# Big products ordered chunk by chunk, so that neighbouring ones write different PSUM banks, in a two-layer hybrid decoder

## The chip, the cores and the metric

The kernel runs on one core of a Trainium2 chip. The metric is the time of one execution on the device in microseconds (us); where several runs are given it is their median.

## What is computed

Two layers over 512 tokens of width 1024, in float32. Each adds to `x` a mixer, a cross attention into 256 memory tokens, and an MLP of hidden width 4096:

```python
for l in range(DEPTH):                      # DEPTH = 2
    h = rmsnorm(x, norm_mix[l])
    x = x + hybrid_mixer(h, w_in[l], ...)   # four branches, gated, w_branch, w_out
    h = rmsnorm(x, norm_xattn[l])
    x = x + cross_attention(h, rmsnorm(mem, norm_mem[l]), w_q, w_kv, w_o)
    h = rmsnorm(x, norm_mlp[l])
    x = x + sq_relu_mlp(h, mlp_w1[l], mlp_w2[l])
return rmsnorm(x, norm_final)
```

Inside the mixer, `h @ w_in` gives the inputs of four token mixers (mLSTM, GLA, S5, HGRN2) and 4096 columns of gates; each branch output is multiplied by its `w_branch`, gated, and summed, and the sum goes through `w_out`. Almost all arithmetic is in the dense products with these weights.

## The kernel before

**Blocks, units, products.** Every dense product is cut into blocks of 256 output columns (`r_f`, `m_o`, `gate2_3`, `q3`, `down3_3` and so on; `block_order` fixes their order). A block over 1024 input rows has four units, a `branch` block (256 input rows) has one. A unit is one DMA of 256 input rows x 256 columns of weights into a ring of nine places. To keep float32 accuracy, each operand is split into a high and a low part: ScalarE (ACT) writes the high part of the weights (line 1135), GpSimd (POOL) subtracts to get the low part (lines 564 and 565), and three products are added: high x high, high weights x low activations, low weights x high activations. A unit holds two chunks of 128 input rows, `k` 0 and 1.

**Banks.** A block accumulates in a set of two PSUM banks, `G[s][0]` and `G[s][1]`; blocks alternate between the two sets (`psum_set`, line 236). In the usual form (`fm`) bank 0 holds output columns 0 to 127 of the block and bank 1 the columns 128 to 255, each with 512 tokens: 12 products of 128x512 per unit, 6 per bank. In the `tm` form (`r_i`, `g_v`, `m_v`, and `kv4` to `kv7`) the activations are stationary, the product is 128x256, and there are four regions of 128 tokens in two banks (two regions for the memory's 256 tokens). `narrow` has a single region.

**The order in `parts` (line 575).** The generator waits for the free set (`gemm_free`, line 581), and in every unit for the weights (`split_ready`). Before: outermost the region `reg`, then the chunk `k`, then the three products. So in the last unit of a block bank 0 gets its last product 6 products before the block's end in `fm` (12 in `tm` over 512 tokens), and `gemm_done` is raised for it there; bank 1's is raised by the last product. Where activations are still being made, `ready` is waited for per chunk, in region 0.

**Who takes the result.** Readers wait for `gemm_done[s]` at `2*used + b + 1`, first b = 0 and then b = 1, and then free the bank: ACT in `banks` (line 1190), `tanh_out` and `gate`, VectorE (DVE) in `merge` (line 1633), in the merge of the fourth branch (line 2058), in `residual` (line 2081) and in `up`. ACT and DVE work through one order written out by hand; ACT also makes the high parts of coming weight units there (`feed_past`, five units ahead of the block's end), and every ACT and DVE instruction waits for the one before it (`chained`). The places that the prediction's steps touch:

- `r_f`: lines 1301 to 1306. ACT copies a bank and takes its absolute value (two instructions per bank), then works on both halves together.
- `m_o`: lines 1378 to 1381, one tanh per bank, followed by the level exponential that a long DVE stretch needs.
- The fourth branch's merge, lines 2058 to 2078: per bank a product with the gate and an addition to `MG`, then two subtractions; ACT makes `MHhi` between them (line 1486). PE runs `branch2_0`, `branch2_1`, `branch2_2` in a row and then `gate2_3`.
- `q3`: line 1515, one copy per bank, then the exponentials of head 0, then `kv_copy(7)`, for which PE waits.
- `down3_3` of the last layer: `residual` adds each bank to `X`, ACT squares and scales (lines 1147 and 1160), DVE sums the squares, and PE's last small products (line 1102 and `norm_tokens`) follow.

Of the kernel before, what the change touches and what calls it, by code (L numbers as in the profile page):

```python
# [13 lines left out]
P = 128  # L14
# [16 lines left out]
BW = 256  # L31
# [104 lines left out]
NARROW = 80  # L136


def units_of(name):
    return 1 if name.startswith("branch") else 4  # L140
# [36 lines left out]
def build(nc, ins, out):  # L177
# [7 lines left out]
    with ctx:  # L185
        def sb(name, shape, dt=F32):
            return ctx.enter_context(nc.sbuf_tensor(name, shape, dt))
# [10 lines left out]
        WLo = nc.alloc_sbuf_tensor_at("w_lo", [P, RING, UW], F32R, offset=ring_at)  # L198
        WHi = sb("w_hi", [P, RING, UW], F32R)
# [33 lines left out]
        def of_layer(s, count):  # L233
            return s, count + now[0] * PER_LAYER[s.name]

        def psum_set(name):
            n = now[0] * NBLOCK + BLOCK[name]
            return n % 2, n // 2

        def first_unit(name):  # L240
            return now[0] * NUNIT + UNIT[name]

        G = [[ctx.enter_context(nc.psum_tensor(f"gemm{s}{b}", [P, 512], F32)) for b in range(2)] for s in range(2)]
# [10 lines left out]
        def sem(name):  # L254
            return ctx.enter_context(nc.semaphore(name))
# [9 lines left out]
        split_hi, split_ready, unit_used = sem("split_hi"), sem("split_ready"), sem("unit_used")  # L265
        gemm_done = [sem(f"gemm_done{i}") for i in range(2)]
# [302 lines left out]
        def _(pe):  # L569
            def mm(o, w, a, start=True, stop=True):  # L570
                return pe.matmul(o, w, a, start=start, stop=stop, skip_group_check=True)  # L571


            def parts(name, hi, lo, kind="fm", n=SEQ, ready=None, ready_at=0):

                s, used = psum_set(name)
                if used:  # L580
                    pe.wait_ge(gemm_free[s], 2 * used)
                u0, units, kcs = first_unit(name), units_of(name), 2
                for un in range(units):
                    u = u0 + un
                    wide = NARROW if kind == "narrow" else BW
                    w_at = lambda W, k, c, m: W[:, u % RING, k * wide + c:k * wide + c + m]
                    nt = {"fm": 2, "tm": n // P, "narrow": 1}[kind]
                    first = True
                    for reg in range(nt):
                        for k in range(kcs):  # L590
                            kc = kcs * un + k
                            if ready is not None and reg == 0:
                                pe.wait_ge(*of_layer(ready, ready_at + kc + 1))
                            if first:
                                pe.wait_ge(split_ready, u + 1)
                                first = False
                            last = kc == kcs * units - 1
                            if kind == "fm":
                                o = G[s][reg][:, 0:n]
                                ops = ((w_at(WHi, k, reg * P, P), hi(kc)), (w_at(WHi, k, reg * P, P), lo(kc)),  # L600
                                       (w_at(WLo, k, reg * P, P), hi(kc)))
                                start = kc == 0
                                ends = last
                            elif kind == "narrow":
                                o = G[s][0][0:NARROW, :]
                                ops = ((w_at(WHi, k, 0, NARROW), hi(kc)), (w_at(WHi, k, 0, NARROW), lo(kc)),
                                       (w_at(WLo, k, 0, NARROW), hi(kc)))
                                start = kc == 0
                                ends = last
                            else:  # L610
                                per = 2 if nt == 4 else 1
                                o = G[s][reg // per][:, (reg % per) * BW:(reg % per) * BW + BW]
                                tok = slice(reg * P, reg * P + P)
                                ops = ((hi(kc)[:, tok], w_at(WHi, k, 0, BW)), (lo(kc)[:, tok], w_at(WHi, k, 0, BW)),
                                       (hi(kc)[:, tok], w_at(WLo, k, 0, BW)))
                                start = kc == 0 and reg % per == 0
                                ends = last and reg % per == per - 1
                            for q, (a, b) in enumerate(ops):
                                i = mm(o, a, b, start=start and q == 0, stop=last and q == 2)
                            if ends:  # L620
                                i.then_inc(gemm_done[s], 2 if kind == "narrow" else 1)

                    if un < units - 1:
                        i.then_inc(unit_used, 1)
                    yield
# [9 lines left out]
            def gemm(*args, **kind):  # L635
                rest(parts(*args, **kind))
# [95 lines left out]
            def gate_parts(n, c):  # L732
                return parts(f"gate{n}_{c}", *H)
# [9 lines left out]
            def x_columns(t, ks, bank):  # L743
                for k in ks:
                    i = pe.transpose(bank(k)[:, t * P:(t + 1) * P], Rf(2 * t + k // 4, 1)[:, (k % 4) * P:(k % 4 + 1) * P], ident)
                return i
# [30 lines left out]
            for L in range(DEPTH):  # L777
                now[0] = L
                block = parts("r_i", *U, kind="tm", ready=u_ready)
                some(block, 2 if L else 1)  # L780
                if L == 0:
                    for k, (s, count) in ((6, (u_hi, 1)), (7, (p_vec, 3))):
                        pe.wait_ge(s, count)
                        for t in range(TT):
                            i = x_columns(t, (k,), XB)
# [86 lines left out]
                for t in range(TT):  # L872
                    i = pe.transpose(M[0][:, t * 64:(t + 1) * 64], R(23)[0:64, 0, t * P:(t + 1) * P], ident[0:64, 0:64])
# [12 lines left out]
                for hp in range(2):  # L886
                    mm(M[hp][:, :], ident, bc(neg_mask, 1, 8), stop=False)
                    for j in range(2):
                        for a in range(2):
                            i = mm(M[hp][64 * a:64 * a + 64, j * 256:j * 256 + 256], head_sel[0:4, 2 * j + hp, :], bm[:, :, a, :],  # L890
                                   start=False, stop=j == 1)
                    i.then_inc(ms["mex_done"], 1)
                for h in range(4):
                    rows = slice(64 * (h % 2), 64 * (h % 2) + 64)
                    for c in range(NCH):
                        tok = slice(c * CH, c * CH + CH)
                        at_ = (h // 2) * 256 + (c // 2) * CH
                        i = mm(M[2 + h % 2][64 * (c % 2):64 * (c % 2) + 64, at_:at_ + CH], MQK[2 + h // 2][rows, tok], MQK[h // 2][rows, tok])
# [3 lines left out]
                for j in range(2):  # L902
                    for t in range(TT):
                        i = pe.transpose(M[j][:, t * P:(t + 1) * P], MQK[2 + j][:, t * P:(t + 1) * P], ident)
# [5 lines left out]
                for h in range(4):  # L910
                    rows = slice(64 * (h % 2), 64 * (h % 2) + 64)
                    for c in range(NCH):
                        p0 = 64 * (c % 2)
                        bank = M[2 * (c % 2) + h // 2]
                        at_ = (c // 2) * 128
                        w = MKT[p0:p0 + 64, c // 2, h // 2, h % 2, :]
                        mm(bank[rows, at_:at_ + 64], w, MV[p0:p0 + 64, c // 2, HD * h:HD * h + HD])
                        i = mm(bank[rows, at_ + 64:at_ + 128], w, ones64[p0:p0 + 64, :])
# [6 lines left out]
                for part in (1, 0):  # L925
# [6 lines left out]
                    for j in range(2):  # L932
                        for c in range(1, NCH):
                            for hp, rows in halves:
                                i = mm(M[2 * part + j][rows, c * CH:(c + 1) * CH], MS[j][rows, c - 1, 64 * part:64 * part + 64],
                                       MQT[rows, j, c * CH:(c + 1) * CH], start=False, stop=True)
# [9 lines left out]
                for r in range(2):  # L946
                    for f in range(2):
                        i = pe.transpose(M[0][:, (2 * r + f) * P:(2 * r + f + 1) * P], R(24 + r)[:, 0, f * P:(f + 1) * P], ident)
                i.then_inc(ss["ct_done"], 1)
                pe.wait_ge(*of_layer(head_rs, 12))  # L950
                for n in range(8):
# [4 lines left out]
                    for t in range(2):  # L956
                        for q in range(2):
                            i = pe.transpose(M[1 + n % 3][:, (2 * t + q) * P:(2 * t + q + 1) * P],
                                             flat(XP[:, r, 4 * q:4 * q + 4, t0 + t, :]), ident)
# [4 lines left out]
                for f in range(2):  # L964
                    for u in range(8):
                        for i4 in range(4):
                            t = 4 * f + i4
                            for r in range(2):
                                i = mm(kk[32 * i4:32 * i4 + 32, f, u, :], XP[:, r, u, t, :], CT[:, r, 32 * t:32 * t + 32],
                                       start=r == 0, stop=r == 1)  # L970
# [8 lines left out]
                un = UU[:, :, :].rearrange("p f (j n) -> p f j n", j=S5_T)  # L979
                for t in range(8):  # L980
                    for r in range(2):
                        at_ = (2 * (t // 4) + r) * 64
                        for q in range(2):
                            for a in range(2):
                                half = slice(64 * a, 64 * a + 64)
                                i = mm(M[t % 4][half, at_:at_ + 64], BT[:, t, r, q, half], U4[:, t, q, :], start=q == 0, stop=q == 1)
# [8 lines left out]
                for f in range(2):  # L995
                    for d in range(S5_T):
                        mm(M[f][:, d * 64:512], KTm[:, f, d, :], flat(un[:, f, 0:S5_T - d, :]), start=d == 0, stop=False)
                    for j in range(S5_T):
                        for i4 in range(4):
                            t = 4 * f + i4  # L1000
                            for r in range(2):
                                i = mm(M[f][32 * i4:32 * i4 + 32, j * 64 + 1:j * 64 + 64], CL[:, r, j, t, :], SX[r][:, t, 0:63],
                                       start=False, stop=r == 1)
# [4 lines left out]
                for n in range(4):  # L1008
                    for k in range(2):
                        i = mm(M[n][:, :], WGLU[:, k, n * P:(n + 1) * P], GE[:, k, :], start=k == 0, stop=k == 1)  # L1010
# [97 lines left out]
            for t in (0, 1):  # L1108
                n = DEPTH * NBLOCK - 2 + t
# [1108 lines left out]
```

## Time and profile before

| | |
|---|---|
| runs | 2127.38, 2127.94, 2133.14 us; median 2127.94 |
| profiled execution | 2130.14 us |
| its span | 2128.3 us, mean granted TensorE clock 0.989 |
| TensorE products | 13631, busy 96% of the span |
| weight loads (PEld) | 13631, busy 79% |
| VectorE, ScalarE, GpSimd | busy 43%, 43%, 49% |

"Busy" of PE counts pipelined products, so that one in flight hides the gap to the next; the distance from start to start is what a stream of products costs. The chain that ended last shows what the end of the span rests on; idle time of an engine matters only where this chain passes it. All products issued through the helper `mm` carry line 571, so they are told apart by their tiles.

### The profile page before, as it was taken

What the parts mean: (1) busy time and instruction counts of PE and PEld (TensorE: products, weight loads), DVE (VectorE), ACT (ScalarE), POOL (GpSimd) and SP (SyncE); (2) the same over time, 40 slices, a digit from 0 to 9 for tenths busy, and PEclk for the clock granted to TensorE, in tenths of its full rate; (3) what the DMA queues carried; (4) which work ended last, traced back from release to release, by engine and by line L of the source; (5) the groups of instructions that cost most, each with busy time, mean ns of one, the idle gap of its engine ahead of it and who ended that gap; (6) DMA issues with size and microseconds to landing.
All of it is one profiled execution on the core that took longest, in us unless ns stands there. A gap on an engine that the chain in (4) does not pass through costs nothing.

```text
span 2128.3 us, 34224 instructions
## 1 busy us (share of the span) xinstructions
PE 2052.3 (96%) x13631; PEld 1689.1 (79%) x13631; DVE 905.7 (43%) x1382; ACT 920.7 (43%) x1568; POOL 1036.7 (49%) x1364
## 2 busy tenths in 40 slices
PE   5999999899999999999999999999999999999998
PEld 4888778777986888888887887777789878888887
DVE  4665765835204321212256576677350243212212
ACT  5655344334445443323356535352345444423323
POOL 2644444444762455456456435426357435555462
PEclk8999999999999999999999999999999999999999
DMA  4322222323431333333333232213224213333332
GB/s 155 98 78 71 75 70 74 86 71 97 135 117 45 94 95 99 97 97 99 95 89 86 67 81 70 69 47 109 85 95 145 94 57 93 99 95 98 97 97 75
DMA packets 205243, 191.21 MB, mean 90 GB/s; under 512 B 30266, under 2 KB 202780, under 8 KB 204700
## 3 DMA queue, kind: packets, MB, share of 16 engines
q1 hardware_dynamic: 205084, 189.02, 30.1%
q8 instruction: 108, 1.77, 0.3%
q14 instruction: 51, 0.42, 0.1%
HBM read 184.77 MB, written 3.15 MB: 88 GB/s over the span
## 4 chain that ended last, share of the span: by engine, by line
PE 83%; DVE 6%; ACT 4%; SPq 3%; issue 1%; POOL 1%; DMA 1%; DVEq 0%; ACTq 0%
PE gemm L571 75%; PE mix L571 7%; SPq L544 2%; DVE work L1593 2%; DVE work L1584 1%; ACT w_hi L1135 1%; DMA small<-in_s_log_step_dram 1%; POOL w_lo L565 1%; DVE work L1680 1%; POOL w_lo L564 0%; DVE work_split L1593 0%; ACT work L1509 0%; DVE merged L1584 0%; SPq L513 0%; DMA w_raw<-in_w_branch_dram 0%
## 5 line engine op out<-in xcount | busy, mean ns | idle before, releaser
L564 POOL TENSOR_TENSOR w_lo<-w_raw,w_hi 128x256 fp32r<-128x256 f32 (+1 forms) x680 | 541.8, 797 | 1064.1 <-ACT w_hi L1135 1063.7
L571 PE MATMUL gemm<-work_split,w_hi 128*128 128x512 f32 (+1 forms) x2048 | 604.5, 379 | 4.7 <-POOL w_lo L565 3.1
L571 PE MATMUL gemm<-h_hi,w_hi 128*128 128x512 f32 (+1 forms) x1456 | 579.6, 398 | 15.5 <-POOL w_lo L565 13.7
L571 PE MATMUL gemm<-h_lo,w_hi 128*128 128x512 f32 (+1 forms) x1456 | 569.2, 391 | 0.0
L571 PE MATMUL gemm<-h_hi,w_lo 128*128 128x512 f32 (+1 forms) x1456 | 568.6, 391 | 0.0
L565 POOL TENSOR_TENSOR w_lo<-w_raw,w_hi 128x256 fp32r<-128x256 f32 (+1 forms) x680 | 543.6, 799 | 0.0
L1135 ACT ACTIVATE w_hi<-w_raw 128x512 fp32r<-128x512 f32 (+1 forms) x680 | 384.3, 619 | 266.3 <-DMA w_raw<-in_mlp_w_dram 186.5
L571 PEld LDWEIGHTS gemm<-work_split,w_hi 128*128 128x128 f32 x2048 | 377.9, 190 | 78.0 <-issue 5.8
L571 PE MATMUL gemm<-work_split,w_lo 128*128 128x512 f32 (+1 forms) x1024 | 386.8, 378 | 0.0
L571 PEld LDWEIGHTS gemm<-h_hi,w_hi 128*128 128x128 f32 (+1 forms) x1456 | 273.6, 188 | 82.4 <-POOL w_lo L565 13.6
L571 PEld LDWEIGHTS gemm<-h_hi,w_lo 128*128 128x128 f32 (+1 forms) x1456 | 273.8, 188 | 59.3
L571 PEld LDWEIGHTS gemm<-h_lo,w_hi 128*128 128x128 f32 (+1 forms) x1456 | 274.0, 188 | 58.0 <-issue 2.4
L571 PEld LDWEIGHTS gemm<-work_split,w_lo 128*128 128x128 f32 x1024 | 194.1, 190 | 35.8
L1584 DVE TENSOR_TENSOR x_t<-x_t,gemm 128x512 f32<-128x512 f32 x96 | 66.0, 688 | 363.4 <-PE gemm L571 362.4
L1584 DVE TENSOR_TENSOR work<-work 128x512 f32<-128x512 f32 (+6 forms) x152 | 127.5, 839 | 69.9 <-ACT work L1226 30.9
L571 PEld LDWEIGHTS mix<-work 64*64 64x64 f32 (+4 forms) x4448 | 114.2, 129 | 38.4 <-issue 31.0
L571 PE MATMUL mix<-work 64*64 64x64 f32 (+6 forms) x4448 | 135.3, 227 | 9.4 <-DVE work L1680 5.1
L1593 DVE SCALAR_TENSOR_TENSOR gate_t<-gemm,work 128x512 f32<-128x512 f32 x64 | 44.3, 692 | 183.5 <-PE gemm L571 165.8
L1559 ACT ACTIVATE gate_t<-gate_t 128x512 f32<-128x512 f32 x64 | 40.5, 632 | 189.1 <-DVE gate_t L1593 189.1
L571 PE MATMUL gemm<-w_hi,work_split 128*128 128x256 f32 x384 | 85.0, 289 | 19.2 <-POOL w_lo L565 19.2
L1220 ACT ACTIVATE gate_t<-gemm 128x512 f32<-128x512 f32 x56 | 33.5, 598 | 124.2 <-PE gemm L571 122.5
L1593 DVE SCALAR_TENSOR_TENSOR work_split<-gate_t,work_split 128x512 fp32r<-128x512 f32 x64 | 46.3, 723 | 91.4 <-ACT work_split L1560 91.4
(278 smaller groups left out, 1674.2 us busy)
## 6 DMA issues: line engine op xcount, KB each, us to landing
w_raw<-in_mlp_w_dram SPq DMA_DIRECT2D x256, 256.0 KB, 2.7
w_raw<-in_w_in_dram SPq DMA_DIRECT2D x224, 256.0 KB, 2.8
w_raw<-in_xattn_w_kv_dram SPq DMA_DIRECT2D x64, 256.0 KB, 2.9
w_raw<-in_w_branch_dram SPq DMA_DIRECT2D x32, 256.0 KB, 2.7
w_raw<-in_w_out_dram SPq DMA_DIRECT2D x32, 256.0 KB, 2.7
w_raw<-in_xattn_w_q_dram SPq DMA_DIRECT2D x32, 256.0 KB, 2.8
w_raw<-in_xattn_w_o_dram SPq DMA_DIRECT2D x32, 256.0 KB, 2.8
work<-in_x_dram SPq DMA_DIRECT2D x4, 512.0 KB, 6.3
```

The source lines that it names most:

```text
L544: sp.dma_start(U4[32 * uu:32 * uu + 32, i4::4, q, :], src).then_inc(ss["u4_in"], 16)
L564: pool.tensor_tensor(lo[:, 0:half], raw[:, 0:half], hi[:, 0:half].bitcast(F32), ALU.subtract)
L565: pool.tensor_tensor(lo[:, half:], raw[:, half:], hi[:, half:].bitcast(F32), ALU.subtract).then_inc(split_ready, 1)
L571: return pe.matmul(o, w, a, start=start, stop=stop, skip_group_check=True)
L1135: act.activation(hi, raw, ACT.Copy).then_inc(split_hi, 1)
L1220: do(act.activation(t[:, b, :], G[s][b][:, :], ACT.Tanh, scale=0.5), th_ready)
L1559: do(act.activation(UPX[1], UPX[0], ACT.Square), up_a)
L1584: do(dve.tensor_tensor(o, a, b, op), s)
L1593: do(dve.scalar_tensor_tensor(out=o, in0=a, scalar=sc, in1=b, op0=op0, op1=op1), s)
L1680: do(dve.copy_predicated(r(m.att[:, b * w:(b + 1) * w]), bc(LM[:, l, :], 1, w // CH), r(bank[:, 0:w])), m.picked)
```

## The change

The loop over regions goes inside: chunk by chunk, and within a chunk product by product (high x high, then weights high x activations low, then weights low x activations high), the regions follow each other. In `fm` banks 0 and 1 alternate; in `tm` with four regions the order is 0, 2, 1, 3, again one bank and the other. The flag that starts a bank goes to the first product of its first region. The `ready` wait stays ahead of a chunk's first product, but all regions of the chunk are now between two such waits. The number of products, their shapes and operands stay. Bank 0's `gemm_done` is raised by its own last product, which is now the last but one of the block (in `tm` with four regions the last but one as well).

```diff
                     nt = {"fm": 2, "tm": n // P, "narrow": 1}[kind]
+                    per = 2 if nt == 4 else 1
                     first = True
-                    for reg in range(nt):
-                        for k in range(kcs):
-                            kc = kcs * un + k
-                            if ready is not None and reg == 0:
-                                pe.wait_ge(*of_layer(ready, ready_at + kc + 1))
-                            if first:
-                                pe.wait_ge(split_ready, u + 1)
-                                first = False
-                            last = kc == kcs * units - 1
...
-                            for q, (a, b) in enumerate(ops):
-                                i = mm(o, a, b, start=start and q == 0, stop=last and q == 2)
-                            if ends:
-                                i.then_inc(gemm_done[s], 2 if kind == "narrow" else 1)
+                    for k in range(kcs):
+                        kc = kcs * un + k
+                        if ready is not None:
+                            pe.wait_ge(*of_layer(ready, ready_at + kc + 1))
+                        if first:
+                            pe.wait_ge(split_ready, u + 1)
+                            first = False
+                        last = kc == kcs * units - 1
+                        for q in range(3):
+                            W, a = ((WHi, hi(kc)), (WHi, lo(kc)), (WLo, hi(kc)))[q]
+                            for at_ in range(nt):
+
+                                reg = (at_ % 2) * 2 + at_ // 2 if nt == 4 else at_
+                                if kind == "fm":
+                                    o, first_of_bank, last_of_bank = G[s][reg][:, 0:n], True, True
+                                    i = mm(o, w_at(W, k, reg * P, P), a, start=kc == 0 and q == 0, stop=last and q == 2)
...
+                                else:
+                                    o = G[s][reg // per][:, (reg % per) * BW:(reg % per) * BW + BW]
+                                    first_of_bank, last_of_bank = reg % per == 0, reg % per == per - 1
+                                    i = mm(o, a[:, reg * P:reg * P + P], w_at(W, k, 0, BW), start=kc == 0 and q == 0 and first_of_bank,
+                                           stop=last and q == 2)
+                                if last and q == 2 and last_of_bank:
+                                    i.then_inc(gemm_done[s], 2 if kind == "narrow" else 1)
```

## Rows read from the trace of the kernel before

**Rows 1.** The page, the chain that ended last: shares by engine.
```profile
PE 83%; DVE 6%; ACT 4%; SPq 3%; issue 1%; POOL 1%; DMA 1%; DVEq 0%; ACTq 0%
```

**Rows 2.** Groups by line and shape, PE: count | busy, mean ns | idle before.
```profile
L571 PE MATMUL gemm<-h_hi,w_hi 128*128 128x512 f32 x1440 | 573.3, 398 | 15.5 <-POOL w_lo L565 13.7 <-DVEq L2068 1.8
...
L571 PE MATMUL gemm<-work_split,w_hi 128*128 128x512 f32 x1792 | 558.4, 393 | 4.7 <-POOL w_lo L565 3.1 <-ACTq L1221 1.6
L571 PE MATMUL gemm<-work_split,w_lo 128*128 128x512 f32 x896 | 350.6, 391 | 0.0
```

**Rows 3.** PE in order of time, a steady stretch: start us, us, what. Twenty-four products.
```profile
1809.69 0.39 PE L571 MATMUL gemm<-h_hi,w_lo 128*128 128x512 f32 x1
1809.91 0.39 PE L571 MATMUL gemm<-h_hi,w_hi 128*128 128x512 f32 x1
1810.14 0.39 PE L571 MATMUL gemm<-h_lo,w_hi 128*128 128x512 f32 x1
1810.37 0.39 PE L571 MATMUL gemm<-h_hi,w_lo 128*128 128x512 f32 x1
...
1811.05 0.39 PE L571 MATMUL gemm<-h_hi,w_lo 128*128 128x512 f32 x1
...
1814.90 0.39 PE L571 MATMUL gemm<-h_lo,w_hi 128*128 128x512 f32 x1
```

**Rows 4.** Windows, PE alone: busy, (count), granted clock, DMA share, GB/s.
```profile
830.00:1000.00 170.00, 170.00 (x752) 1.00 0.32 98
1126.00:1130.00 4.00, 3.94 (x17) 1.00 0.00 0
1538.80:1545.00 6.20, 6.15 (x15) 0.52 0.00 0
```

**Rows 5.** PE in order of time, a `tm` block: three products per 0.36 us.
```profile
1604.80 0.28 PE L571 MATMUL gemm<-work_split,w_lo 128*128 128x256 f32 x1
```

**Rows 6.** ACT in order of time around the end of `r_f`, first layer.
```profile
70.11 0.60 ACT L1302 ACTIVATE work<-gemm 128x512 f32<-128x512 f32 x1 [2.97 <-PE gemm L571]
70.74 0.60 ACT L1303 ACTIVATE work<-gemm 128x512 f32<-128x512 f32 x1
71.47 0.60 ACT L1302 ACTIVATE work<-gemm 128x512 f32<-128x512 f32 x1
```

**Rows 7.** ACT in order of time around the end of `m_o`, first layer.
```profile
203.21 0.60 ACT L1379 ACTIVATE work<-gemm 128x512 f32<-128x512 f32 x1 [6.40 <-PE gemm L571]
204.57 0.60 ACT L1379 ACTIVATE m_out_gate<-gemm 128x512 f32<-128x512 f32 x1 [0.76 <-PE gemm L571]
```

**Rows 8.** DVE in order of time, the merge of `branch2_0`, first layer.
```profile
482.39 0.69 DVE L1593 SCALAR_TENSOR_TENSOR gate_t<-gate_t,gemm 128x512 f32<-128x512 f32 x1 [8.45 <-PE gemm L571]
484.17 0.69 DVE L1593 SCALAR_TENSOR_TENSOR gate_t<-gate_t,gemm 128x512 f32<-128x512 f32 x1 [0.25 <-DVEq L2070]
```

**Rows 9.** ACT in order of time around the end of `q3`, first layer.
```profile
640.70 0.60 ACT L1515 ACTIVATE merged<-gemm 128x512 f32<-128x512 f32 x1 [0.76 <-PE gemm L571]
```

**Rows 10.** DVE in order of time at the end of the kernel.
```profile
2114.15 0.69 DVE L1584 TENSOR_TENSOR x_t<-x_t,gemm 128x512 f32<-128x512 f32 x1 [7.79 <-PE gemm L571]
...
2117.99 0.69 DVE L1584 TENSOR_TENSOR work<-work,gate_t 128x512 f32<-128x512 f32 x1 [0.75 <-ACT gate_t L1147]
```

**Rows 11.** The chain that ended last, where it comes back to PE: start us, us, what.
```profile
87.62 2.56 PE gemm L571 x10
...
246.32 0.63 PE mix L681 x4
...
498.77 11.43 PE gemm L571 x42
...
647.19 3.73 PE gemm L571 x16
...
2118.79 1.01 PE mix L571 x8
```

**Rows 12.** Who waited for whom, PE alone: us in total, times, longest us.
```profile
PE gemm L571 <- POOL w_lo L565: 36.0, 13, 15.3
```

More of the change, by code:

```diff
@@ L587, in parts @@
                     nt = {"fm": 2, "tm": n // P, "narrow": 1}[kind]
+                    per = 2 if nt == 4 else 1
                     first = True
-                    for reg in range(nt):
-                        for k in range(kcs):
-                            kc = kcs * un + k
-                            if ready is not None and reg == 0:
-                                pe.wait_ge(*of_layer(ready, ready_at + kc + 1))
-                            if first:
-                                pe.wait_ge(split_ready, u + 1)
-                                first = False
-                            last = kc == kcs * units - 1
[L598 to L617, printed above, removed]
-                            for q, (a, b) in enumerate(ops):
-                                i = mm(o, a, b, start=start and q == 0, stop=last and q == 2)
-                            if ends:
-                                i.then_inc(gemm_done[s], 2 if kind == "narrow" else 1)
@@ new lines, in parts @@
+                    for k in range(kcs):
[13 more added lines that the diff above has]
+                                    i = mm(o, w_at(W, k, reg * P, P), a, start=kc == 0 and q == 0, stop=last and q == 2)
+                                elif kind == "narrow":
+                                    o, first_of_bank, last_of_bank = G[s][0][0:NARROW, :], True, True
+                                    i = mm(o, w_at(W, k, 0, NARROW), a, start=kc == 0 and q == 0, stop=last and q == 2)
+                                else:
[5 more added lines that the diff above has]
+                                    i.then_inc(gemm_done[s], 2 if kind == "narrow" else 1)
```

## The prediction

> **What bounds the kernel now.** I read the chain that ended last first: TensorE (PE) holds 83% of it [rows 1]. So the span is the stream of products, plus the places where PE waits. The groups by shape then say what the stream is made of: the five groups of 128x512 products with split weights hold 3 x 1440 + 1792 + 896 = 7008 products [rows 2]. Their mean of 391 to 398 ns is no cost, since products overlap; the cost is the distance between starts. In order of time a steady stretch shows starts at 1809.69 and 1814.90 with 23 steps between them, 226.5 ns each [rows 3], and a window of 170 us holds 752 products, 226 ns each, at a granted clock of 1.00, the 2.4 GHz level [rows 4]. In a `tm` block three 128x256 products take 0.36 us, 120 ns each [rows 5]. Half the columns thus save 106.7 ns, so 512 columns stream in 213.3 ns and 13.3 ns of each product are a fixed part. That fixed part is what "different banks" could remove.
>
> The waits come next. PE waits 36.0 us in 13 places for a low part from POOL [rows 12], but POOL is only the last link: the chain goes back from POOL to ACT, which makes the high part when its hand-written order lets it, and from there to whatever ACT or DVE work stood ahead. I followed each such stretch back to the PE instruction that it began with. Chains that come back to PE in front of a wait of PE begin, in each layer, at the ends of `r_f`, `m_o`, `branch2_0` and `q3`, and one more at the end of the last block [rows 6 to 11]. The others begin at small products, at SyncE's 32 copies for the S5 branch or inside attention, which the change leaves alone.
>
> **The change, part by part.**
>
> *Banks alternate.* The old order already changes banks, at every sixth product. A unit is 12 products, so the 23 steps of [rows 3] hold four or so changes of bank beside 19 repeats, and all of them are 0.22 or 0.23 us: no step is the 0.21 that a product without its fixed part would take. The mean over 752 products says the same. I take 0 for this part. The bounds: if each product gave back 13.3 ns, 7008 of them would give 93 us, and some 1000 `tm` products 13 us more; in the other direction, a change of bank costs nothing in the rows, so the bound below is nothing. I take the value at the end where the rows lie, since these steps are the very event, only rarer.
> The Trainium skill (TensorE: Matmul & The Clock Gate, section Back-to-back issue gap) gives 512/2.4 + 2.5 = 216 ns for such a product alone. By an estimate from that page the room above its floor would be 226.5 - 216 = 10.5 ns, or 74 us over 7008 products; it does not say what holds it.
>
> *Operands.* Before, the high weights were used twice in a row, now the same activations are. Each product has its own weight load either way, and the step after a repeated weight is as long as the others [rows 3]. 0 us, hidden under the product in flight; were that cover gone, it would show in every step.
>
> *`ready` waits.* PE now has six products instead of three between two waits for chunks, and three fewer behind the last one (0.68 us). This pays only where PE stands at such a wait. None of the 13 waits is one: the stages that use it begin with two or more units whose chunks were made before, and unit 3 comes 36 products, 8.2 us, after the block's start. 0 us; at most 0.7 us in one place.
>
> *Bank 0 is finished later.* This is the part with a price. In `fm` bank 0's last product was 6 from the end and is now 1 from it: 5 x 226.7 = 1.13 us later. Bank 1's time stays. In steady stages the next use of the set is a whole block (10.9 us) away and the cover holds. On the five chains it does not:
>
> 1. `r_f`. ACT had bank 0 at 70.11 and needs two instructions for it; bank 1's began at 71.47, 1.36 us later [rows 6]. Now bank 0 begins at 71.24, the pair takes two times 0.63 and about 0.07 to the next, and bank 1 begins at 72.57: 1.10 us later. All that follows on ACT and DVE moves, up to PE at 87.62 [rows 11]. Twice: 2.2 us.
> 2. `m_o`. One tanh per bank, and ACT idled 0.76 us between them [rows 7], which covers part: 1.13 - 0.76 = 0.37 us. The DVE stretch behind it ends at PE's 246.32 [rows 11]. Twice: 0.74 us.
> 3. `branch2_0`. DVE waited 8.45 us for bank 0, and from there it runs without a break worth 0.3 us; it came to bank 1 at 484.17, when that was long done [rows 8]. All 1.13 us go through: `gate2_3` starts later (its set is freed later) and the weights for its third unit come later still, PE goes on at 498.77 [rows 11]. The two waits stand in one chain, so they count once. Twice: 2.27 us. If ACT had had weights ready, only the first would be left.
> 4. `q3`. As 2: one copy per bank and 0.76 us of idle time ahead of bank 1's [rows 9]; 0.37 us up to PE at 647.19 [rows 11]. Twice: 0.74 us.
> 5. The end. DVE takes bank 0 at 2114.15 and ends its last sum at 2117.99 + 0.69 = 2118.68; PE's last products start 0.1 us later [rows 10, 11]. Everything there moves by 1.13 us. Once: 1.13 us.
>
> Sum: 2.2 + 0.74 + 2.27 + 0.74 + 1.13 = 7.1 us. Against the profiled execution's own 2130.14 us that is 2137.2 us. The median of the runs is 2127.94, 2.2 us under it, and to this I add the same 7.1: **2135.0 us**.
>
> What no row shows is a wait that does not exist yet because the slack was under 1.1 us. From below it is 0. From above I allow one per layer, 2.3 us, the size of item 3. I take 0, because the long idle times of ACT and DVE ahead of other blocks' ends (6 to 9 us in [rows 7, 8, 10]) are nearer to slack than to none.
>
> **The rivals.**
>
> *A. The delays are partly absorbed.* The chains have links that I took as rigid; ACT may be ahead with the weights. For it: items 2 and 4 are small, and item 1 rests on the spacing of two short instructions. If only the two kinds with DVE in one piece remain (items 3 and 5), the sum is 2.27 + 1.13 = 3.4 us: 2131.3 us. That is no change, since about 0.3% (6.4 us) is what a measurement of this kernel can tell.
>
> *B. The fixed part is a cost of the same bank, and shows only when banks alternate product by product.* The mechanism would sit at each product start, and it decides if it gives back more than 7.1 us / 7008, or 1 ns per product, less than the timeline of the trace resolves in one step. If all 13.3 ns went, the time would be 2135 - 106 = 2029 us; if a quarter, 2108 us. Against it: the changes of bank in [rows 3] cost what the repeats cost. Only an effect that needs two changes in a row would escape these rows. This is the case on the faster side.
>
> *C. Longer waits bring low clock.* After the longest wait in the `branch2` stretch of the second layer the granted clock is 0.52, near the 1.2 GHz level, and 15 products take 6.15 us, where 3.4 would do [rows 4]: 2.7 us. After the wait that ends at 1126 it stayed at 1.00. The waits of items 1 and 3 become some 1.1 us longer. Two more such stretches: 2135.0 + 5.4 = 2140.4 us.
>
> *D. Alternating unsettles the clock in the steady stages.* The rows show 170 us at 1.00 with a change of bank every sixth product and no idle time [rows 4]. If a tenth of the 7008 products ran at the rate of the slow stretch, 0.41 us instead of 0.227, that would be 128 us: 2263 us. For it speaks no row: nothing in the new order makes PE idle in a stream.
> The Trainium skill (TensorE: Matmul & The Clock Gate, section A second HAM failure mode: psum-queue depth-cycling) speaks against this change: it tells of a kernel that cycled through PSUM banks every iteration, idled briefly between groups, and had its clock go up and down. By that rule, D; the trace disagrees so far, with 1.00 where banks already change.
>
> **How the numbers follow.** The forecast (the five chains, 7.1 us) gets 0.52. Its sum is close above 6.4 us, so 0.40 of it is slower by over 0.3% and 0.12 within. A gets 0.26, all within. B gets 0.07, faster. C gets 0.12 and D 0.03, slower. Faster 0.07, same 0.38, slower 0.55. The range: below, A's 2131.3 less about 2 us for the spread of the runs (2127.38 to 2133.14), 2129.5; above, C's 2140.4 and half a us, 2141, which also takes in the two unseen waits. B and D, 0.10 together, are left out. The predicted time is the forecast's, 2135.0 us.
>
> **What would show it.** The steps of a steady stretch stay at 0.22 and 0.23 us and the 170 us window still holds about 752 products: then B and D are out. ACT's second bank at the end of `r_f` starts some 1.3 us after the first, back to back, and no longer waits for PE; the idle 0.76 us ahead of bank 1 at `m_o` and `q3` is gone; DVE's first merge of `branch2_0` starts 1.1 us later against the block's end. PE's waits for POOL grow from 36.0 us by some 4 to 5, the rest lies in the waits for small products and in the tail, where the time from the last big product to the end grows by 1.1 us. The prediction is wrong if the step from start to start changes at all, by even 1 ns, or if PE's waits for POOL do not grow.

## The result: 2149.3 us, slower by 0.8%

| | kernel before | changed kernel |
|---|---|---|
| median | 2129.01 us (2127.38 to 2133.14, 4 runs) | 2149.30 us (2147.22 to 2150.22, 4 runs) |
| ratio | 1 | 1.008, 95% interval 1.0068 to 1.0092 |
| profiled execution, span | 2130.14, 2128.3 us | 2149.47, 2147.4 us |
| granted clock, mean | 0.989 | 0.984 |

The direction was forecast, the size was not: 20.3 us more where 7.1 were predicted, and the time lies outside the stated range.

The stream itself did not change. In order of time, a steady stretch of the changed kernel: products now come in pairs, one per bank, which the view joins into one row (x2) with the start of the first.

```profile
1833.62 0.62 PE L571 MATMUL gemm<-h_hi,w_lo 128*128 128x512 f32 x2
1834.07 0.62 PE L571 MATMUL gemm<-h_hi,w_hi 128*128 128x512 f32 x2
1834.53 0.61 PE L571 MATMUL gemm<-h_lo,w_hi 128*128 128x512 f32 x2
...
1835.89 0.61 PE L571 MATMUL gemm<-h_lo,w_hi 128*128 128x512 f32 x2
```

Ten products from 1833.62 to 1835.89 are 227 ns each, as in [rows 3]. The window of 170 us, moved by 20 us so that it lies in the same stage, holds 752 products again, the number of [rows 4]:

```profile
850.00:1020.00 170.00, 170.00 (x752) 1.00 0.31 97
```

One line of the page could mislead here. The group by line and tiles answers to the one of [rows 2] (with one more form):

```profile
L571 PE MATMUL gemm<-h_hi,w_hi 128*128 128x512 f32 (+1 forms) x1456 | 463.0, 398 | 19.8 <-POOL w_lo L565 15.9
```

Busy falls from 579.6 us for the same group before to 463.0, yet the mean of one stays 398 ns: neighbours of one group overlap, and an overlap is counted once. It says how products are grouped, not how fast they are.

So the time was not lost in the steady stream. Who waited for whom, PE alone, in the changed kernel:

```profile
PE gemm L571 <- POOL w_lo L565: 39.9, 15, 14.5
...
PE gemm L571 <- DVEq L2062: 3.9, 2, 1.9
...
PE gemm L571 <- ACT work L1491: 2.5, 2, 1.3
PE mix L571 <- DVE work L1578: 2.2, 5, 0.9
PE mix L952 <- DVE work L1578: 1.5, 2, 0.8
```

The waits for POOL are 15 instead of 13 [rows 12], and 39.9 us instead of 36.0.

Both kernels issue the same number of products in the same order of blocks, so product n of one trace can be set against product n of the other, and the difference of their start times shows where time is lost. For the first pair of profiles, each start counted from the start of its span, the difference is 19.2 us at the last product. These places have a longer wait:

| place (what waits) | first layer | second layer | predicted, each |
|---|---|---|---|
| after `r_f` (third block after it, weights) | 1.12 | 1.13 | 1.10 |
| after `m_o` (small products, then the last GLA level) | 0.46 | 0.49 | 0.37 |
| transposes for S5 | 0.41 | 0.44 | not seen |
| `branch2_0` (`gate2_3` starts) | 1.14 | 1.13 | 1.13 |
| `branch2_3` (`out1` starts) | 0.83 | 0.79 | not seen |
| `q3` (attention starts) | 0.49 | 0.50 | 0.37 |
| first `down3_3` (sum of squares) | | 0.61 | not seen |
| last `down3_3`, end of the kernel | | 1.14 | 1.13 |

These sum to 4.45 + 6.23 = 10.7 us. That leaves 8.5 us. By the same start times some 7 us of it, net, are products that run at the low clock level in one of the two executions only: in the changed kernel near 295, 678, 1135, 1466 and 1729 us, 1.4 to 1.7 us each, while the kernel before loses more near 1540 us. Another 1.8 us are a longer wait near 1466 us, for low parts that POOL made slowly. The rest are small: two places of 0.2 us each near 565 and 1616 us, and a shorter wait behind the prologue, which gives 0.5 us back. Windows of PE in the changed kernel:

```profile
1135.00:1140.00 5.00, 4.49 (x14) 0.66 0.00 0
676.00:684.00 8.00, 6.24 (x16) 0.79 0.00 1
295.00:299.50 4.50, 4.50 (x14) 0.62 0.00 2
```

and the same places in the kernel before:

```profile
1126.00:1131.00 5.00, 4.94 (x22) 1.00 0.14 32
670.00:678.00 8.00, 5.80 (x19) 1.00 0.00 1
293.60:298.00 4.40, 4.40 (x20) 1.00 0.09 13
```

In 4.5 us 14 products ran where 20 did in 4.4. The attention's stretch costs 1.70 us by the start times, and there is one in each layer. The wait near 1466 us, first the kernel before, then the changed one:

```profile
1451.88 0.70 PE L571 MATMUL gemm<-work_split,w_hi 128*128 128x512 f32 x2 [0.92 <-POOL w_lo L565]
...
1455.49 0.47 PE L571 MATMUL gemm<-h_hi,w_hi 128*128 128x512 f32 x1 [0.63 <-POOL w_lo L565]
```

```profile
1465.97 1.91 PE L571 MATMUL gemm<-work_split,w_hi 128*128 128x512 f32 x4 [3.50 <-POOL w_lo L565]
```

**The chain at `r_f`, as predicted.** ACT in order of time, changed kernel; it answers to [rows 6]:

```profile
70.75 0.60 ACT L1296 ACTIVATE work<-gemm 128x512 f32<-128x512 f32 x1 [4.41 <-PE gemm L571]
71.38 0.60 ACT L1297 ACTIVATE work<-gemm 128x512 f32<-128x512 f32 x1
72.10 0.60 ACT L1296 ACTIVATE work<-gemm 128x512 f32<-128x512 f32 x1
72.73 0.60 ACT L1297 ACTIVATE work<-gemm 128x512 f32<-128x512 f32 x1
```

Its second bank begins 1.35 us after the first, right behind the pair of instructions of the first, and no longer when PE ends. Before, ACT's wait ahead of bank 0 was 2.97 us, now it is 4.41. In the fourth branch, DVE has a break of 9.58 us ahead of `branch2_0` where it had 8.45 [rows 8]: 1.13 us more. Then PE, at the start of `gate2_3`, first the kernel before, then the changed one:

```profile
489.94 0.50 PE L571 MATMUL gemm<-h_hi,w_hi 128*128 128x512 f32 x1 [0.89 <-DVEq L2068]
```

```profile
494.42 0.73 PE L571 MATMUL gemm<-h_hi,w_hi 128*128 128x512 f32 x2 [1.94 <-DVEq L2062]
...
503.25 0.92 PE L571 MATMUL gemm<-h_hi,w_hi 128*128 128x512 f32 x2 [3.10 <-POOL w_lo L565]
```

The wait at 503.25 is as long as it was (3.09 us): the two stand in one chain and count once.

**The wait that was not there.** POOL and PE in the kernel before, at the start of `out1`:

```profile
518.07 0.92 POOL L565 TENSOR_TENSOR w_lo<-w_raw,w_hi 128x256 fp32r<-128x256 f32 x1
...
519.55 0.62 PE L571 MATMUL gemm<-work_split,w_hi 128*128 128x512 f32 x2
```

and in the changed kernel:

```profile
523.70 0.91 POOL L565 TENSOR_TENSOR w_lo<-w_raw,w_hi 128x256 fp32r<-128x256 f32 x1
...
524.76 0.94 PE L571 MATMUL gemm<-work_split,w_hi 128*128 128x512 f32 x3 [0.55 <-POOL w_lo L565]
```

In the changed kernel PE waits for this low part and begins 0.15 us after POOL's end at 524.61. Before, POOL ended at 518.99 and PE came to this unit at 519.55, 0.56 us later. So there was no idle time of PE to read, and the slack was only 0.4 us: of a delay of 1.13 us some 0.7 became a wait. The chain is `branch2_3`'s merge on DVE, the high parts of `MG` and of the memory on ACT, and only then the weights.

### The profile page after: what moved, and what is told of

Read it like the earlier page. It is cut to its first block, busy times and chain, and to the rows that moved or that the text cites. A ratio compares the mean times of both kernels' runs of the same rounds, so it can differ in the third digit from the quotient of the medians.

```text
span 2147.4 us, 34224 instructions
## 1 busy us (share of the span) xinstructions
PE 2062.1 (96%) x13631; PEld 1695.0 (79%) x13631; DVE 898.2 (42%) x1382; ACT 918.5 (43%) x1568; POOL 1036.4 (48%) x1364
## 4 chain that ended last, share of the span: by engine, by line
PE 81%; DVE 8%; ACT 5%; SPq 2%; POOL 1%; issue 1%; DMA 1%; DVEq 0%; ACTq 0%
PE gemm L571 74%; PE mix L571 7%; DVE work L1587 2%; DVE work L1578 2%; SPq L544 1%; ACT w_hi L1129 1%; POOL w_lo L565 1%; POOL w_lo L564 1%; DMA small<-in_s_log_step_dram 1%; DVE work_split L1587 1%; DVE merged L1578 1%; DVE work L1674 1%; DVE work L1582 0%; ACT work L1503 0%; DMA w_raw<-in_w_branch_dram 0%
## 5 line engine op out<-in xcount | busy, mean ns | idle before, releaser
L571 PE MATMUL gemm<-work_split,w_hi 128*128 128x512 f32 (+1 forms) x2048 | 530.1, 381 | 6.5 <-POOL w_lo L565 5.6
L571 PE MATMUL gemm<-h_hi,w_hi 128*128 128x512 f32 (+1 forms) x1456 | 463.0, 398 | 19.8 <-POOL w_lo L565 15.9
L571 PE MATMUL gemm<-h_lo,w_hi 128*128 128x512 f32 (+1 forms) x1456 | 452.4, 391 | 0.0
L571 PE MATMUL gemm<-h_hi,w_lo 128*128 128x512 f32 (+1 forms) x1456 | 451.3, 390 | 0.0
L571 PEld LDWEIGHTS gemm<-h_hi,w_hi 128*128 128x128 f32 (+1 forms) x1456 | 269.2, 188 | 85.6 <-POOL w_lo L565 15.8
L571 PE MATMUL gemm<-work_split,w_lo 128*128 128x512 f32 (+1 forms) x1024 | 304.0, 378 | 0.0
L571 PE MATMUL gemm<-w_hi,work_split 128*128 128x256 f32 x384 | 64.5, 291 | 18.4 <-POOL w_lo L565 18.4
```

## The experiments

Each kernel was timed together with the kernel before. That kernel's own median differs from one such group of runs to the next by up to 5 us (2129 to 2133.6), so the ratio is what counts.

**1. Only the signal late, the order old.**

```diff
                             for q, (a, b) in enumerate(ops):
                                 i = mm(o, a, b, start=start and q == 0, stop=last and q == 2)
-                            if ends:
+                                if late and last and reg == nt - 1 and q == 1:
+                                    i.then_inc(gemm_done[s], 1)
+                            if ends and (not late or reg == nt - 1):
                                 i.then_inc(gemm_done[s], 2 if kind == "narrow" else 1)
```

`late` is true for every block but `narrow`.

> Old order of the products; only the signal for bank 0 is raised on the last but one product of each block, as in the changed kernel. Theory T (the whole loss comes from bank 0 being reported 5 products later; the order itself costs nothing): within 2 us of the changed kernel's 2149 us, and PE's wait in front of the second unit pair of gate2_3 about 2.3 us as there. Rival O (alternating banks costs something by itself): near 2129 us, the kernel before.

Measured: 2151.5 us against 2131.0, ratio 1.0097 (1.0082 to 1.0113). The steady stream is that of the kernel before. Two rows of its waits, for weights and, the second, for a free set of banks (`gemm_free`) at the start of `gate2_3`:

```profile
PE gemm L571 <- POOL w_lo L565: 36.3, 16, 14.6
...
PE gemm L571 <- DVEq L2071: 3.9, 2, 2.0
```

The second row is the changed kernel's 3.9 us to the tenth. All of the loss is there with the old order. Rival O, that alternating the banks costs something by itself, is not needed. The expectation named the wait of the wrong unit ("second unit pair"): the 2 us stand at the start of `gate2_3`. The prediction had said that PE's waits for POOL would grow by 4 to 5 us; here they grow by 0.3 and the time still by 20, so that sum was a poor test: it also holds the wait behind the prologue (15.3 to 14.6 us at its longest) and the one near 1466 us. That it grew by 3.9 us in the changed kernel is in part luck, since 2 us of that are slow low parts of POOL.

**2. New order in all units but the last,** which is as in the kernel before (shown against that kernel's loops).

```diff
+                    if un == units - 1:
+                        for reg in range(nt):
+                            for k in range(kcs):
...
+                    else:
+                        for k in range(kcs):
...
+                            for q in range(3):
...
+                                for at_ in range(nt):
...
```

> New order in every unit but the last of a block, which has the old order, so that bank 0 is again reported 6 products before the end; the one-unit branch blocks are thereby wholly old. Most products still alternate banks. Theory T: 2127 to 2131 us, the kernel before. Rival O: about three quarters of the loss stays, 2144 us.

Measured: 2131.6 us against 2131.0, ratio 1.0005 (0.9996 to 1.0014). Three quarters of a full block's products alternate banks and nothing is gained or lost. The window of 170 us:

```profile
850.00:1020.00 170.00, 170.00 (x752) 1.00 0.31 96
```

**3. New order, but the old one in the last unit of six blocks.** As 2, with `un == units - 1 and name in ("r_f", "m_o", "branch2_0", "branch2_3", "q3", "down3_3")`.

> Changed kernel, with the old order in the last unit of six blocks only: r_f, m_o, branch2_0, branch2_3, q3, down3_3. Theory T with these six as the whole list: 2128 to 2132 us. If other blocks matter as well (the wait for the sum of squares at the start of the second layer, the waits for small products), 2133 to 2140 us. Rival O: 2147 us or more.

Measured: 2135.8 us against 2131.0, ratio 1.0022 (1.0011 to 1.0032): 4.8 us stay, 15 of about 20 are gone. The six are most of the list but not all of it; by start times the transposes for S5 still cost 0.4 us in each layer. The profile also has a stretch of low clock near 294 us (1.6 us) and slow weights near 415 us (2.8 us with the low clock behind them). These two need not come from the change: run 2, which loses nothing, has low clock near 294 us as well and waits 3.41 us for slow weights near 1459 us. So most of the 4.8 us is not accounted for.

**4. Late signal in `r_f` alone.** The edit of 1 with `late` true for `r_f` only.

> Kernel before, with the late signal for bank 0 in r_f alone (one block per layer). The chain alone gives 2 x 1.1 = 2.2 us: 2131 us. If longer waits also bring stretches of low clock, as in the changed kernel's second layer at 1136 us, up to 1.4 us more for each, in that place or in others that are only shifted: 2131 to 2135 us, with the granted clock in the window after that wait near 0.5.

Measured: 2134.6 us against 2131.0, ratio 1.0013 (1.0004 to 1.0022). By start times the first layer's wait is 1.11 us longer, the second layer's place 2.59, of which some 1.5 are slow products after it. The chain alone would be 2.2 of the 3.6 us; the interval of the ratio is 0.9 to 4.7 us and holds it.

**5. Late signal in `branch2_0` and `branch2_3`.**

> Kernel before, with the late signal for bank 0 in branch2_0 and branch2_3 alone. The chains of the changed kernel give 1.13 us for branch2_0 and 0.8 us for the wait in out1 behind branch2_3, twice each: 3.9 us over the kernel before of the same call, plus or minus 2 us of low clock. If branch2_0's delay were absorbed by weights that are ready, 1.6 us.

Measured: 2139.4 us against 2133.6, ratio 1.0027 (1.0017 to 1.0037), 5.8 us. By start times 1.14 and 0.79 us in the first layer, 1.13 and 0.79 in the second: 3.85 us, the expected 3.9. The full 1.13 us of `branch2_0` go through. The interval of the ratio, 3.6 to 7.9 us, holds this value, so the medians do not show that anything more was lost. The profiled execution is 10.1 us longer than the first one of the kernel before, and beside the 3.85 us it has attention's low stretch in the first layer (1.69 us), though nothing in or right before attention was changed, another such stretch near 294 us (1.6 us), and 3.3 us near 1460 us, where PE waits 3.44 us for slow low parts.

**6. Late signal in the six blocks.** The complement of 3.

> Kernel before, with the late signal in r_f, m_o, branch2_0, branch2_3, q3 and down3_3: the complement of the run that gave these six the old order. If the six carry nearly all of the loss: 14 to 18 us over the kernel before. If the loss is spread over all blocks, about 10 us.

Measured: 2148.7 us against 2133.6, ratio 1.0067 (1.0054 to 1.0080), 15.1 us. With 3, the six carry some three quarters of the loss. This profile too has a wait of 3.54 us for slow low parts near 1465 us.

**7 and 8. Both kernels again, one profile each.**

> The kernel before, unchanged, for a second profile. If the stretches of low clock are the same in every execution, they stand at the same products (near 241, 500, 1278, 1333 and 1538 us). If they partly fall by chance, some are elsewhere, attention at 670 or 1710 us among them, and the time is within 2127 to 2136 us.

> The changed kernel, unchanged, for a second profile. If its ten stretches of low clock follow from its longer waits, most are there again, the ones after the wait at 1135 us and in both attentions among them; if they were chance, their number falls towards the six or seven of the kernel before.

Measured: 2132.8 and 2147.8 us. The waits of the table come back within 0.1 us almost everywhere (the S5 transposes within 0.2) and sum to 10.5 us, of a difference of spans of 15.1. So only 4.6 us are left in this pair, against 8.5 in the first: some 3.3 us of low clock, net, and 1.1 us of a longer wait for slow low parts near 418 us. The long wait near 1466 us is not there: the second profile of the changed kernel has 1.25 us in its place. The kernel before has other stretches this time. It runs slowly near 295 us, as the changed kernel does:

```profile
294.70:298.00 3.30, 3.30 (x8) 0.50 0.00 0
```

Attention in its second layer, in the second profile and then in the first:

```profile
1712.00:1720.00 8.00, 6.24 (x16) 0.79 0.00 0
```

```profile
1709.00:1717.00 8.00, 5.99 (x25) 1.00 0.00 0
```

The stretches that both executions of the changed kernel have in these two places can thus hit the kernel before as well. The changed kernel's own places came back, in its second profile:

```profile
676.00:684.00 8.00, 6.10 (x17) 0.79 0.00 1
1135.00:1140.00 5.00, 3.64 (x9) 0.67 0.00 0
```

**9. A shift without a longer wait.**

```diff
+                    if name == "q0" and un == 1:
+                        pe.wait_ge(split_ready, u + 1)
+                        for _ in range(5):
+                            mm(M[3][:, :], ident, reset)
```

> Kernel before, with five fp32 products of 128x512 (0.43 us each) more in the second unit of q0 of each layer, written to a bank that is overwritten later. No wait grows; what follows is only 2.1 us later. If low clock in attention depends on where its short idle times fall and not on longer waits, the stretch near 672 us (first layer) or 1713 us (second) can be there now, worth 1.7 us each: 4.3 us for the products plus 0 to 3.4 us. If low clock needs a longer wait, the sum is 4.3 us exactly and attention shows none.

Measured: 2144.6 us against 2132.6, ratio 1.0054 (1.0042 to 1.0065). My size for the filler was wrong: one fp32 product of 128x512 takes 0.86 us and stands as two entries of 0.43. Ten of them are 8.7 us, and 3.3 of the 12 us are left, within the expected 0 to 3.4. Attention's second layer has the stretch, its first has not: it comes and goes with no change to any wait.

**10 and 11. Fillers in the waits, twice too long.** Products of constants ahead of the waits, to keep PE busy:

```diff
+                    if name == "gate2_3" and un == 2:
+                        fill(M[1], 6)
+                    if name == "r_q" and un == 0:
+                        fill(G[s][0], (2, 6)[now[0]])
...
+                s_, used_ = psum_set("branch3_2")
+                pe.wait_ge(gemm_free[s_], 2 * used_)
+                fill(G[s_][0], 5)
                 scores(gl, 6)
```

> Kernel before, with filler products (constants, written to banks that are overwritten later) in front of three waits of PE: 2 and 6 in r_q, 5 before the last level of GLA scores, 6 before the third unit of gate2_3. They end before the waited-for work does. If the slow products after these waits come from the idle time, the granted clock stays at 1.00 near 241, 500, 1280 and 1540 us and the kernel gains about 6 us over the kernel before; if the clock falls for another reason, no change or a loss of 1 us.

> Changed kernel with the same fillers (4 and 8 in r_q, where it waits longer). Its waits stay, its low clock after them goes: 2149 us less 6 to 8 us, 2141 to 2143 us, the chain part of the loss alone being left. If the clock had no part in the loss, 2149 us.

Measured: 2139.4 us (ratio 1.0036, 1.0022 to 1.0049) and 2155.4 us (1.0108, 1.0095 to 1.0122) against 2132.6. Both lose. The mean clock rises to 0.991 in both, but the fillers end after the work that PE waits for, and those in `r_q` stood where there is no wait: the long one comes in `g_qk`. They say nothing on whether low clock is part of the loss.

**12 and 13. The same, sized by measurement.** Two products ahead of `scores(gl, 6)`, three in `gate2_3`, none in `r_q`; in the changed kernel four more ahead of the second unit of the second layer's `g_qk`.

> Kernel before, with fillers sized by what the last fillers took (0.86 us for each fp32 product of 128x512, which stands as two entries in the trace): 2 in front of the last level of GLA scores (1.7 us of a wait of 2.5), 3 in front of the third unit of gate2_3 (2.6 us of 3.1), none elsewhere. They end inside the wait, so they cost nothing; the low clock after these waits goes (1.6 to 2.8 us each). Gain of 3 to 6 us over the kernel before. If low clock only moves to other places, no gain.

> Changed kernel, with the same fillers and 4 in the second layer's g_qk, in front of its second unit (3.4 us of a wait of 4.1). Chains as in the changed kernel, low clock less: 3 to 8 us under the changed kernel, 11 to 15 us over the kernel before. If low clock has no part in the loss, no difference to the changed kernel (about 17 us over).

Measured: the kernel before with fillers 2135.2 us against 2131.7, ratio 1.0018 (1.0010 to 1.0027), slower, where a gain was expected. The changed kernel with them 2146.5 us, ratio 1.0067 (1.0054 to 1.0079), 2 to 3 us less than without (1.008), with intervals that overlap; the single run 8 of the unchanged kernel lies at 1.0067 too, so no gain is shown. In the trace of 12 the fillers do what they should in their own place. PE in order of time, then two windows:

```profile
498.66 2.74 PE L571 MATMUL mix<-consts_sb 128*128 128x512 f32 x6
501.92 0.50 PE L571 MATMUL gemm<-h_hi,w_hi 128*128 128x512 f32 x1 [0.52 <-POOL w_lo L565]
```

```profile
502.00:508.00 6.00, 6.00 (x27) 1.00 0.13 44
288.00:300.00 12.00, 11.87 (x36) 0.72 0.16 43
```

The six entries are three products; PE then still waits 0.52 us, and the products after the wait run at 1.00. But low clock stands in other places, where no filler was, and the sum is a loss. One is near 290 us (1.00 in the first profile of the kernel before, low in the second). Another follows the second layer's wait behind `r_f`, which is as long as in the kernel before:

```profile
1127.59 0.50 PE L571 MATMUL gemm<-h_hi,w_hi 128*128 128x512 f32 x1 [2.57 <-POOL w_lo L565]
```

```profile
1128.50:1131.90 3.40, 3.40 (x10) 0.50 0.02 5
```

That the fillers moved the low clock there is not shown, since such stretches come and go without them.

## Why the prediction was wrong in size

**The bound, and the fixed part of a product: right.** The steps stayed at 227 ns in the changed kernel and in run 2, so rival B is out. That the old changes of bank cost what the repeats cost was the right row to read. Rival D as well: 1.00 over the 170 us. The Trainium skill (TensorE: Matmul & The Clock Gate, A second HAM failure mode: psum-queue depth-cycling) tells of a clock that goes up and down in a kernel that cycles through banks and idles briefly between groups of products. In the steady stages here PE alternates banks without idling, and the clock stays at 1.00 over the 170 us, so the change of bank alone does not do it; the idle time of that rule was not tried.

**Bank 0 later as the cause: right, and shown both ways.** With the old order and the late signal all of the loss is there (run 1), with the new order in all but the last unit, and the signal early again, none of it (run 2, 1.0005).

**The five chains: right, two undersized.** `r_f` 1.12 for 1.10, `branch2_0` 1.14 for 1.13, the end 1.14 for 1.13. Behind one tanh or copy per bank, I let the 0.76 us that ACT idled cover that much of the delay, but each instruction also takes its own hand-over to the next. At `m_o` the two tanhs, 0.60 us each, start 0.72 us apart when nothing keeps them (204.97 and 205.69 in the changed kernel), and were 1.36 us apart before. So 0.64 us was cover, and 1.13 - 0.64 = 0.49 us go through, as PE's waits show at `q3` (0.49 and 0.50) and, split over two waits, at `m_o` (0.46 and 0.49). Together 7.6 us for 7.1.

**The step that failed first: "What no row shows is a wait that does not exist yet ... I take 0".** It was 3.1 us in the first pair of profiles (2.8 in the second): 1.6 behind `branch2_3`, 0.85 at the S5 transposes, 0.6 at the sum of squares. The bound of 2.3 us that I had given was too low as well. The reason for taking 0, long idle times of ACT and DVE ahead of other blocks, was the wrong row: idle time before a block's end says nothing of the slack behind it. Behind `branch2_3` that slack was 0.4 us. The row to read is when POOL ended a low part and when PE began the product with it.

**The step that failed second: low clock at 0.** Rival C had low clock at 5.4 us and a chance of 0.12. By start times it was some 7 and 3.3 us, net, in the two pairs of profiles. What I took for the exception is part of the difference. Against the forecast of 7.1 us stand 10.7 us of longer waits, this low clock, and, in the first pair alone, 1.8 us of slow low parts. Rival C's own reason, that longer waits bring low clock, is not shown.

**What is not settled.** That slow products and slow low parts make up the difference between 10.7 us of waits and some 15 to 20 us in all is read from the traces; no run removes them alone. The wait for slow low parts near 1466 us is scatter as far as the profiles go: it is about 3.5 us in the changed kernel and in runs 2, 5 and 6, one of which loses nothing, and 0.9 to 1.3 us in the kernel before, run 7 and run 8. Why the changed kernel has more low clock is not shown either. One stretch goes with the late signals: attention's in the first layer stands in all seven profiles in which `branch2_0` and `branch2_3` signal late (both of the changed kernel, runs 1, 5, 6, 11 and 13) and in none of the eight others. Yet attention's waits are as long as before, so a longer wait does not explain it. The stretch behind `r_f` in the second layer, with a wait of 3.7 us where there were 2.6, came in all four executions profiled with all or six signals late and no filler, in run 4 too, and also in runs 9 and 12, where that wait was not touched. Others vary between executions of one kernel.

No version beat the kernel before; run 2 equals it.

## What to carry to other kernels

When the order inside a block is changed, look at which product completes each result and who waits for it: here the order itself cost nothing and a signal 1.13 us later, at every block, cost 20 us in 2130. A delay on a chain is paid again at every place where the chain has no slack, and slack is not read from idle time but from how close the producer's end stands to the consumer's start. To tell an order from its signals, keep the one and move the other; it takes two runs.

## What the runs showed that I had not expected

- A fp32 product of 128x512 stands as two entries, 0.86 us in all, while the split form's three products take 0.68 us: a count of entries is not a count of instructions.
- Stretches at the low clock level come in executions of one unchanged kernel in different places (attention's second layer in one of two profiles of the kernel before), each worth some 1.4 to 1.7 us, and with one wait filled they stood in other places.
- POOL's low part took 2.74 us instead of 0.73 in some places, in the kernel before as well (at 409.65 and 1451.73 us). The chain of the changed kernel near 1466 us, in front of the longest wait of its second layer but one:

```profile
1460.22 2.88 POOL w_lo L564
1463.10 2.74 POOL w_lo L565
1465.97 2.33 PE gemm L571 x5
```
